# Two weight loads instead of three for a product in split precision: gate/up, down and out projections

## The reference, cut to what matters

```python
def _swiglu(x, w_gate_up, w_down):
    gate, up = jnp.split(x @ w_gate_up, 2, axis=-1)
    return (jax.nn.silu(gate) * up) @ w_down
...
        x = _layernorm(ALPHA * x + h, ln_g[i, 0], ln_b[i, 0])      # h: the mixer's output
        x = _layernorm(ALPHA * x + _swiglu(x, ffn_w_gate_up[i], ffn_w_down[i]), ln_g[i, 1], ln_b[i, 1])
```

## Time and profile before

| | us |
|---|---|
| median of 3 runs | 2294.64 |
| lowest, highest | 2290.96, 2296.02 |
| span of the profiled execution | 2291.1 |
| TensorE busy in it | 2220.8 |
| VectorE busy | 1617.0 |
| ScalarE busy | 1153.3 |

### The profile page before, as it was taken

How to read it: one execution, slowest core, us unless ns; L and a number is a source line. 1 busy time by engine, 2 the same in 40 slices (tenths; PEclk the granted TensorE clock), 3 DMA queues, 4 the chain that set the end, 5 groups by cost and what they waited for, 6 DMA issues and landing times.

```text
span 2291.1 us, 41288 instructions
## 1 busy us (share of the span) xinstructions
PE 2220.8 (97%) x17284; PEld 2045.5 (89%) x17284; DVE 1617.0 (71%) x2739; ACT 1153.3 (50%) x1927; POOL 153.4 (7%) x142
## 2 busy tenths in 40 slices
PE   7999999999989999999999999999999999999998
PEld 3665889998879999999999989997779999999998
DVE  4389668555977555788557787577988557799654
ACT  2425445344365345766335664345556345957343
POOL 0013000000000000000000000015630000000000
PEclk9999999999999999999999999999999999999999
DMA  8148154555244554514554425562025554514552
GB/s 346 59 185 317 47 221 166 184 184 202 93 159 172 185 184 166 185 56 168 184 183 166 147 93 203 184 221 75 19 93 184 185 184 168 184 55 166 184 185 92
DMA packets 50729, 368.46 MB, mean 161 GB/s; under 512 B 5616, under 2 KB 5744, under 8 KB 6384
## 3 DMA queue, kind: packets, MB, share of 16 engines
q1 hardware_dynamic: 50400, 363.72, 43.6%
q10 hardware_dynamic: 144, 2.10, 0.2%
HBM read 364.75 MB, written 1.05 MB: 160 GB/s over the span
## 4 chain that ended last, share of the span: by engine, by line
PE 80%; DVE 11%; ACT 5%; issue 2%; DMA 1%; SPq 0%; DVEq 0%; POOL 0%; ACTq 0%
PE psum L262 67%; DVE weight_rest L256 2%; PE psum L4430 1%; PE psum L2991 1%; PE psum L4431 1%; DMA weight_ring<-stream_dram 1%; ACT weight_parts L220 1%; PE psum L4452 1%; PE psum L3625 1%; PE psum L2641 1%; DVE work L1943 1%; PE psum L4466 1%; DVE work L3455 1%; DVE spare L2431 0%; DVE work L2430 0%
## 5 line engine op out<-in xcount | busy, mean ns | idle before, releaser
L262 PE MATMUL psum<-input_parts,weight_parts 128*128 128x256 f32 x5184 | 931.6, 283 | 6.0 <-DVE work L1488 1.8
L262 PEld LDWEIGHTS psum<-input_parts,weight_parts 128*128 128x128 f32 x5184 | 799.7, 189 | 11.2 <-issue 5.3
L262 PE MATMUL psum<-input_parts,weight_rest 128*128 128x256 f32 x2592 | 732.9, 283 | 0.0
L256 DVE TENSOR_TENSOR weight_rest<-weight_ring,weight_parts 128x1024 fp32r<-128x1024 f32 x528 | 621.0, 1221 | 152.6 <-ACT weight_parts L220 152.2
L220 ACT ACTIVATE weight_parts<-weight_ring 128x1024 fp32r<-128x1024 f32 x540 | 538.1, 1051 | 130.9 <-PE psum L262 106.9
L262 PEld LDWEIGHTS psum<-input_parts,weight_rest 128*128 128x128 f32 x2592 | 488.1, 188 | 0.0
L262 PE MATMUL psum<-hidden_parts,weight_parts 128*128 128x256 f32 x2496 | 450.8, 283 | 2.6 <-DVE weight_rest L256 1.2
L262 PEld LDWEIGHTS psum<-hidden_parts,weight_parts 128*128 128x128 f32 x2496 | 385.1, 189 | 5.9 <-issue 3.4
L262 PE MATMUL psum<-hidden_parts,weight_rest 128*128 128x256 f32 x1248 | 352.3, 282 | 0.0
L262 PEld LDWEIGHTS psum<-hidden_parts,weight_rest 128*128 128x128 f32 x1248 | 235.0, 188 | 0.0
L1472 ACT ACTIVATE work<-psum 128x256 f32<-128x256 f32 x118 | 45.2, 383 | 352.0 <-PE psum L262 349.6
(11 more groups left out here) (523 smaller groups left out, 2834.7 us busy)
## 6 DMA issues: line engine op xcount, KB each, us to landing
weight_ring<-stream_dram SPq DMA_DIRECT2D x341, 1024.0 KB, 4.8
constants<-constants_dram SPq DMA_DIRECT2D x1, 2304.0 KB, 14.5
work<-s_bc_dram ACTq DMA_DIRECT2D x1, 2048.0 KB, 11.3
work<-ctx_dram SPq DMA_DIRECT2D x1, 1024.0 KB, 6.6
residual<-x_dram SPq DMA_DIRECT2D x1, 1024.0 KB, 8.6
out_dram<-residual SPq DMA_DIRECT2D x4, 256.0 KB, 2.1
vectors<-vectors_dram SPq DMA_DIRECT2D x1, 550.5 KB, 3.8
constants<-constants_dram SPq DMA_DIRECT2D x1, 64.0 KB, 3.5
```

What stands on the lines that cost most here:

```text
L256: ins = dve.tensor_tensor(self.rest[:, i % RING, cols], self.ring[:, i % RING, cols], self.parts[:, s % SPLITS, cols].bitcast(F32), ALU.su ...
L262: mm = pe.matmul(*args, **kw)
```

## The change

`product_in_halves` replaces `product` in gate/up (from the first slab that isn't raw), in columns 0 to 5 of the mixers' out projections, and in columns 0 to 6 of the down projections. (S5's gated out projection, the mixers' input projections and the raw slabs stay.) It issues two matmuls: the rounded weight by rounded input and rest side by side, 512 columns over the whole bank, and the weight's rest by the rounded input, 256 columns added onto the second half. The bank's first half then holds one term, the second the other two, and somebody has to add the halves.

In gate/up a slab now takes two adjoining banks (a pair never wraps around the end of the seven; one is skipped if it would). ScalarE copies the second halves of both banks out (512 columns), VectorE adds the first halves to them, ScalarE takes silu, VectorE multiplies; the banks are free after the addition. In the out projections VectorE has one more addition of 256 columns for each such column (`add_half`); groups of two columns take two banks. In `OutProjection` ScalarE's square of such a column is taken from SBUF, behind the addition and behind the next group's rounding of slabs (`square_whole`).

```diff
+    def product_in_halves(self, pe, bank, w, x, start, stop):
+
+        both = bank.rearrange("p (s t) -> p s t", s=2)
+        self.matmul(pe, both, w[0], x, start=start, stop=False)
+        return self.matmul(pe, both[:, 1, :], w[1], x[:, 0, :], start=False, stop=stop)
...
+    def job_in_adjoining_banks(self, free):
+
+        if self.jobs % BANKS == BANKS - 1:
+            self.jobs += 1
+        b = self.jobs % BANKS
+        job = self.job_in_two_banks(free)
+        job.banks = self.psum[:, b:b + 2, :]
+        return job
...
+        self.halved = 6 if self.chunks == KC else 7
...
+            if n < self.halved:
+                mm = k.weights.product_in_halves(pe, bank, w, self.x.both(c), at == 0, at == self.chunks - 1)
+            else:
+                mm = k.weights.product(pe, bank[:, 0:T], w, self.x.each(c), at == 0, at == self.chunks - 1)
...
+    def square_whole(self, act, c):
+
+        act.wait_ge(*self.y_whole[c])
+        act.activation(self.sq[:, c, :], self.y[:, c, :], ACT.Square).then_inc(self.y_squared[c][0], 1)
+
+    def add_half(self, dve, bank, c):
+
+        dve.wait_ge(*self.y_ready[c])
+        dve.tensor_tensor(self.y[:, c, :], self.y[:, c, :], bank.ap[:, T:2 * T], ALU.add).then_inc(self.y_whole[c][0], 1)
...
+            if g[0]:
+                for c in self.groups[self.groups.index(g) - 1]:
+                    if c < self.halved:
+                        self.square_whole(act, c)
             act.wait_ge(*job.full)
...
             k.weights.split_through(dve, k.weights.ahead(last, 2))
+            for c in g:
+                if c < self.halved:
+                    self.add_half(dve, job if c == g[-1] else job.early, c)
...
+    def add_half(self, dve, bank, c):
+
+        y = self.y[:, c, :]
+        done = self.y_late[c - LATE] if c >= LATE else self.y_ready[c]
+        dve.wait_ge(*self.y_half[c])
+        dve.tensor_tensor(y, y, bank.ap[:, T:2 * T], ALU.add).then_inc(done[0], 1)
+        if c >= LATE:
+            dve.wait_ge(*done)
...
+        self.jobs = [k.job_in_two_banks(free) for free in self.whole[0:self.wide]]
+        self.jobs += [k.job_in_adjoining_banks(free) for free in self.added[self.wide:]]
...
-            act.activation(self.hid[:, j % 2, :], job.early.ap[:, 0:T], ACT.Silu).then_inc(self.silu[j][0], 1)
+            both = self.both[:, j % 2, :, :]
+            act.activation(both, job.banks[:, :, T:2 * T], ACT.Identity).then_inc(self.copied[j][0], 1)
+            act.wait_ge(*self.added[j])
+            act.activation(both[:, 0, :], both[:, 0, :], ACT.Silu).then_inc(self.silu[j][0], 1)
...
+                both = self.both[:, j % 2, :, :]
+                dve.wait_ge(*self.copied[j])
+                dve.tensor_tensor(both, both, job.banks[:, :, 0:T], ALU.add).then_inc(self.added[j][0], 1)
                 dve.wait_ge(*self.silu[j])
-                dve.tensor_tensor(hid, hid, job.ap[:, T:2 * T], ALU.mult).then_inc(self.whole[j][0], 1)
+                hid = both[:, 0, :]
+                dve.tensor_tensor(hid, hid, both[:, 1, :], ALU.mult).then_inc(self.whole[j][0], 1)
```

More of the change, by code:

```diff
@@ L273, in product, with __init__, __getitem__, both @@
         return mm
+    def product_in_halves(self, pe, bank, w, x, start, stop):
+        both = bank.rearrange("p (s t) -> p s t", s=2)
+        self.matmul(pe, both, w[0], x, start=start, stop=False)
+        return self.matmul(pe, both[:, 1, :], w[1], x[:, 0, :], start=False, stop=stop)
+class Parts:
+    def __init__(self, whole):
+        self.whole = whole
+    def __getitem__(self, part):
+        return self.whole[:, part, :, :]
+    def both(self, c):
+        return self.whole[:, :, c, :]
+    def each(self, c):
+        return [self.whole[:, part, c, :] for part in range(2)]
 class Core:
@@ L796, in setup, with columns @@
         self.root_free, k.root_free = k.root_free, self.h_new[-1]
-    def columns(self, pe, out, n):
+    def columns(self, pe, bank, n):
         k = self.k
@@ L955, in first_columns @@
         for i, (job, half) in enumerate(columns):
-            mm = k.weights.product(pe, job.ap[:, half * T:(half + 1) * T],
-                                   [s[:, c, i % 2 * P:(i % 2 + 1) * P] for s in slabs[i // 2]],
-                                   [part[:, c, :] for part in x], at == 0, at == KC - 1)
+            w = [s[:, c, i % 2 * P:(i % 2 + 1) * P] for s in slabs[i // 2]]
+            if halves:
+                mm = k.weights.product_in_halves(pe, job.ap, w, x.both(c), at == 0, at == KC - 1)
+            else:
+                mm = k.weights.product(pe, job.ap[:, half * T:(half + 1) * T], w, x.each(c), at == 0, at == KC - 1)
             if at == KC - 1 and job.full:
@@ L1033, in setup, with columns @@
         self.root_free, k.root_free = k.root_free, self.h_new[-1]
-    def columns(self, pe, out, n, pause=None):
+    def columns(self, pe, bank, half, n, pause=None):
         k = self.k
@@ L1051, in columns @@
                 pause(pe)
-            mm = k.weights.product(pe, out, w, [x[:, c, :] for x in self.x], c == 0, c == self.chunks - 1)
+            if n < self.halved:
+                mm = k.weights.product_in_halves(pe, bank, w, self.x.both(c), c == 0, c == self.chunks - 1)
+            else:
+                mm = k.weights.product(pe, bank[:, half * T:(half + 1) * T], w, self.x.each(c), c == 0,
+                                       c == self.chunks - 1)
         return mm
```

169 lines of the change are left out of this document (96 added, 73 removed).

## The result

| us | before | after |
|---|---|---|
| median of 7 runs | 2295.58 | 2302.07 |
| lowest, highest | 2290.96, 2296.49 | 2300.47, 2305.3 |
| span of the profiled execution | 2291.1 | 2300.2 |

The changed kernel is slower: ratio 1.004, 95% interval 1.0031 to 1.005, which is some 9 us (7 to 11.5); the two medians are 6.5 us apart. The forecast of 2251 and its range of 2230 to 2290 were wrong, and so was the sign.

What follows compares the result with a forecast made beforehand. TensorE's matmul count times pitch was taken as the bound: 70.2 us gained less 26.8 of waits is 43; the span of 2291.1 less 43 plus 3.5 gives 2251 us, range 2230 to 2290.

Steps and rivals of the forecast that it cites:

- The product: In all changed projections, one product falls from 358 to 335 ns; 3052 products gain 70.2 us if TensorE never waits.
- Rival 1: The 8 ns excess belongs to every fp32r matmul: product 343 ns, gain 46 us, net 19, time 2275 us; 13%.
- rival 2: Load already hidden or 512-column matmul split: product stays 358 ns, 27 us of waits remain, time 2321 us; 14%.
- point of decision: Waits of 27 us over 3052 products are 9 ns each: above 349 ns a product the kernel gets slower.
- bound of 0 to 31 ns: Gain per product: 0 if 512 columns cost twice the present pitch, 31 ns if all waiting went.
- Rival 3: In gate/up, the ScalarE and VectorE chain takes over from TensorE at 5.76 us a slab: time 2298 us; 8%.
- starts of the RMS layers: Slab 3's up half waits for slab 0's bank and the clock falls: 4.4 us in two layers, 8.8 (5.4 to 12).
- starts of the LN layers: Only in ln1, slab 3 lies wholly on slab 0's banks and waits for them: 2.2 us.
- LN mixers' out: In hgrn0, mlstm and hgrn1, six VectorE additions delay the sum of squares: 2.4 us each, 7.2 in all.
- down projections: At the ends in ln0, ln1 and ln2, three additions make the sum of squares some 1.9 us later: 5.7 in all.
- hybrid and conformer: In their out projections, moved squares and additions add about .7 us and the 1.1 gain is lost: 2.9 in all.
- The chain in gate/up: VectorE's chain grows to 4.7 us a slab, hidden behind TensorE's 5.36 with .6 us of room: cost 0.

Runs made afterwards that it cites:

- blocks of one form: The kernel before, with blocks of 48 independent fp32r matmuls added behind its last matmul: pitches of 120 ns for 256 columns, 227 for 512.
- slab3_as_before: The changed kernel, but slab 3 of the two RMS layers in the old one-bank form: 2297.57 us, ratio 1.0016 to the kernel before.
- picked: The kernel before, new form only in gate/up (not slab 3 of RMS layers) and down of RMS layers, ln1, ln3: 2281.95 against 2293.32 us, ratio 0.9947.
- out_only: The kernel before, with only the five mixers' out projections and the six down projections changed: 2304.56 us, ratio 1.0041.
- mixers_two: The changed kernel, but only columns 0 and 1 in the new form in the three LN mixers' out projections: 2300.76 us, ratio 1.0032.

## Why the prediction was wrong, by its own steps

**The product (the step that failed).** "An fp32r matmul of 512 columns streams as long as a plain one of 256, and then the load behind it is covered: 216." It took 230 in the kernel and 227 in a block of its own. The 8 ns that a 256 lies above 111 were read as a late load, which a longer stream would cover; the runs show that 512 columns keep 11 to 14 ns above the plain record's 216, with a full load or a small one. And the 111 of the plain 128-column record, which served as the bare streaming time, is itself about the least pitch that a load of 128 x 128 allowed (112 with 128 fp32r columns). So the nearest rows had other limits than the matmul they stood for. Whether the remainder belongs to the columns or to each matmul stays open (the two readings above). The gain was 1762 products x 4.9 (RMS and ln2 layers, mixers, and the two later columns of the other down projections) + 1290 x 8.9 (gate/up and five columns of down in ln0, ln1, ln3) = 8.6 + 11.5 = 20.1 us instead of 70.2. This 50 is nearly the whole error of 51.

**The rivals.** What came lies between two of them. Rival 1 (the excess belongs to every fp32r matmul: 224 + 119 = 343) had 13%; rival 2 (the column rate is what one sees: 238 + 119 = 358) had 14%. The blocks of one form, 227 + 120 = 347, are nearer to rival 1; the kernel's 351.1 lies past the point of decision of 349, on rival 2's side, and there the sign was lost. Rival 2's own price, no gain at all, was too high: with 358 - 351.1 = 6.9 ns a product, 21 us, its sum gives 2321 - 21 = 2300. The bound of 0 to 31 ns held the value; the choice within it did not. The range, which ended at 2290, left out rival 2 and all between. Rival 3 did not come: the chain had 1.06 us of room a slab.

The rule weighed there, N/2.4 + 2.5 ns, which the Trainium skill (TensorE: Matmul & The Clock Gate, Back-to-back issue gap) gives as the isolated gap of one matmul, had warned that little could be won: 2.5 ns a product where 4.9 or 8.9 came. Its gaps, 215.8 and 109.2, were not reached by any fp32r matmul here (226.7 and 113.3 at the least, with steady starts).

**The waits.** Measured as a stage's difference plus the gain of its own products:

| term | predicted | measured |
|---|---|---|
| starts of the RMS layers | 8.8 | 2.8 + 3.2 + 3.0 = 9.0 |
| starts of the LN layers | 2.2 (ln1 alone) | 1.4 + 1.7 + 1.3 + 1.0 = 5.4 |
| LN mixers' out | 7.2 | 6.3 + .7 = 7.0 |
| down projections | 5.7 | 1.3 + 1.0 + 1.6 + .3 = 4.2 |
| hybrid and conformer | 2.9 | 2.5 + 1.4 + .2 + .1 + .2 = 4.4 |
| sum | 26.8 | 30.0 |

20.1 - 30.0 is 9.9 us slower, by construction the sum of the stage differences; the profiled spans differ by 9.1, since a fall of the clock at 2046 us is missing in the later one (1.6) and what lies before the hybrid's out projection took .9 longer. That the sum of the waits came near its forecast is in part luck: LN starts and the hybrid were priced too low, the down projections too high.

- RMS starts: right in place, wait (3.77 us against 4) and clock; slab3_as_before shows the cause in the first layer, picked in both.
- LN starts: the count of banks found the wait on a raw slab's bank in ln1 (.7) and missed 1.1 in ln0. In ln2 and ln3 TensorE waits 1.4 and .8 for a late split (L256), which the prediction had called hidden.
- LN mixers: the additions are the cause, but not at the place named. Today's sum of squares is not what comes late; TensorE stops at the sum of columns 0 to 3 (L1204) and at the first raw input (L1265), where the kernel before had no wait but .3 in mlstm. The sum agrees by luck: 1.3 of lateness and 1.1 of lost gain a mixer were forecast, 2.0 to 2.4 and .2 came.
- Down projections: right in kind, but the wait that grew is for the sum of the later columns (.24 to 1.60 in ln0), not for the sum of squares behind it (.46 as before); somewhat high.
- The chain in gate/up was hidden, as priced, but for the late splits at the starts of ln2 and ln3.
- Hybrid: the moved squares and the additions made the stage 2.5 later, not .7. In its trace ScalarE first idles for an addition, and then, behind a rounding of 2 us (L220), its squares (L918) are what VectorE's sum waits for:

```profile
334.35 0.42 ACT L918 ACTIVATE work<-work 128x256 f32<-128x256 f32 x1 [1.24 <-DVE work L923]
...
340.32 0.69 DVE L959 TENSOR_TENSOR work<-work 128x512 f32<-128x512 f32 x1 [1.28 <-ACT work L918]
```

How the 2.5 us divide between the two was not taken apart. The longer idle time (1.41, 1.00 and 2.85 us instead of 1.19 and 1.58) was followed in after and in out_only by a stretch at the lower clock, 1.4 us that the sum did not have. In slab3_as_before and mixers_two, with the same hybrid stage, the clock fell 4 us earlier, inside the idle time (at 346 us), and the raw slabs lost nothing.

## What to carry to other kernels

Before a pitch is split into streaming and waiting, find a row in which one of the two is really absent, and see that the row isn't at a limit of its own; where no such row stands in the trace, carry both bounds (here 216 and 2 x 119.3 = 239; 227 to 230 came) instead of choosing one. Merging matmuls bought only a part of a load, here 5 to 9 ns of 356 to 360, so every wait that the merge adds elsewhere must be priced against that. And take such a change stage by stage: the same edit gained up to 1.8 us in a gate/up stage whose banks were free and lost 3 where one wasn't.

## What was not expected of the hardware

- fp32r matmuls of 256, 384 and 512 columns with weights of 128 output columns took 120, 173.3 and 226.7 ns. At 0.417 ns a column, half of plain fp32's 0.833, that leaves 13.3 ns a matmul, where plain matmuls of 256 and 512 columns (215.8 and 429.2) leave 2.5. With weights of 64 output columns, 256 columns took 113.3 and the pair of 512 and 256 took 340, 0.443 a column. What makes up the difference is open.
- A product of three has two steady paces, 356.0 and 360.0 ns, that hold for a whole gate/up stage: in the first the starts repeat 115, 117, 122, 120, 119, in the second 120, 122, 118. In the down projections of ln0, ln1 and ln3 the pace goes from 360 to 356 where two other matmuls (L1133) come in behind column 4. In the form of after the pace is the same in all six layers' gate/up stages. What chooses the pace was not found; it makes the gain differ by a factor of nearly two between layers.
- With weights of 64 output columns, 512 columns in a row took 230 ns, more than with 128 (227), while in pairs with a 256 they took 227.
